# Two units of an output projection computed as one block with two sets of seven products

## The reference

```python
y = _rms(h, norm_mix_g[i])
z = y @ w_in[i]                       # 2048 x 4096
za, zb, zc, zd = jnp.split(z, split_at, axis=-1)
oa = _mixer_sgu(za, ...)              # spatial gating, 512 wide
ob = _mixer_shortconv(zb, sc_conv_w[i])
oc = _mixer_conformer(zc, ...)
od = _mixer_pool(zd, pool_w[i], pool_scale[i])
h = h + jnp.concatenate([oa, ob, oc, od], axis=-1) @ w_out[i]    # 2048 x 2048
y = _rms(h, norm_ffn_g[i])
h = h + (jax.nn.silu(y @ w_gate[i]) * (y @ w_up[i])) @ w_down[i]
...
h = h + jax.nn.sigmoid(y @ w_ple_gate[i]) * (p[i] @ w_ple_proj[i])
```

## Time and profile before

| | us |
|---|---|
| median of 3 runs | 1378.53 (1377.76 to 1378.97) |
| the profiled execution | 1376.73 |
| its span, first to last instruction | 1375.0 |
| TensorE busy (6169 matmuls) | 1369.3 |
| VectorE busy | 1156.1 |
| ScalarE busy | 885.2 |
| GpSimd busy | 151.3 |

### The profile page before, as it was taken

The page is one execution under the profiler, slowest core; times in us unless marked ns, Lnnn a source line. Parts: engine busy times, 40 slices in busy tenths (PEclk is TensorE's granted clock), DMA queues, the critical chain, the costliest instruction groups (busy, mean ns, idle before and its releaser), DMA issues.

```text
span 1375.0 us, 16935 instructions
## 1 busy us (share of the span) xinstructions
PE 1369.3 (100%) x6169; PEld 1122.6 (82%) x6169; DVE 1156.1 (84%) x1332; ACT 885.2 (64%) x1181; POOL 151.3 (11%) x129
## 2 busy tenths in 40 slices
PE   9999999999999999999999999999999999999998
PEld 7888888888888888888888888888888887777887
DVE  5589986687999988899999889988766769886898
ACT  7476755576777555777756576756666656665554
POOL 2000010011111000111100011100000144430000
PEclk9999999999999999999999999999999999999999
DMA  9776648887999788999987889998987878889686
GB/s 329 252 212 216 201 158 283 278 242 241 296 279 261 234 257 253 271 269 265 281 262 251 254 253 244 284 290 241 310 312 270 278 242 260 257 265 281 210 251 174
DMA packets 183146, 352.93 MB, mean 257 GB/s; under 512 B 13105, under 2 KB 37933, under 8 KB 182936
## 3 DMA queue, kind: packets, MB, share of 16 engines
q1 hardware_dynamic: 160408, 291.66, 64.5%
q0 software_dynamic: 9568, 35.02, 13.2%
q10 hardware_dynamic: 13088, 25.18, 6.1%
HBM read 296.19 MB, written 27.31 MB: 235 GB/s over the span
## 4 chain that ended last, share of the span: by engine, by line
PE 99%; DVE 0%; DMA 0%; ACT 0%; issue 0%; SPq 0%
PE acc L2216 14%; PE acc L2397 14%; PE acc L2400 14%; PE acc L2399 14%; PE acc L2217 14%; PE acc L2218 14%; PE sp L2400 2%; PE sp L2399 2%; PE tp L2400 2%; PE tp L2399 2%; PE sp L2397 2%; PE tp L2397 2%; PE acc L2278 1%; PE sp L2517 1%; PE tp L2533 1%; PE tp L2236 0%
## 5 line engine op out<-in xcount | busy, mean ns | idle before, releaser
L979 ACT ACTIVATE w_hi<-w_raw 128x1024 fp32r<-128x1024 f32 x451 | 472.1, 1056 | 294.8 <-PE acc L2218 188.0
L1419 DVE TENSOR_TENSOR w_lo<-w_raw,w_hi 128x1024 fp32r<-128x1024 f32 x429 | 519.1, 1225 | 131.6 <-ACT w_hi L979 128.7
L2216 PE MATMUL acc<-w_lo,hh 128*128 128x512 f32 x480 | 189.0, 394 | 0.0
L2218 PE MATMUL acc<-w_hi,hl 128*128 128x512 f32 x480 | 186.9, 389 | 0.0
L2217 PE MATMUL acc<-w_hi,hh 128*128 128x512 f32 x480 | 186.9, 389 | 0.0
L2397 PE MATMUL acc<-w_lo,yh 128*128 128x512 f32 x452 | 176.0, 389 | 0.0
L2399 PE MATMUL acc<-w_hi,yh 128*128 128x512 f32 x452 | 175.9, 389 | 0.0
L2400 PE MATMUL acc<-w_hi,yl 128*128 128x512 f32 x452 | 175.9, 389 | 0.0
L979 ACT ACTIVATE w_hi<-wide 128x1024 fp32r<-128x1024 f32 x108 | 114.3, 1060 | 69.6 <-DVE wide L1433 30.2
L1419 DVE TENSOR_TENSOR w_lo<-wide,w_hi 128x1024 fp32r<-128x1024 f32 x108 | 131.5, 1222 | 14.9 <-ACT w_hi L979 14.6
L2216 PE MATMUL acc<-w_lo,yh 128*128 128x512 f32 x352 | 137.4, 390 | 0.0
(11 more groups left out here) (333 smaller groups left out, 2227.6 us busy)
## 6 DMA issues: line engine op xcount, KB each, us to landing
w_raw<-in_w_gate SPq DMA_DIRECT2D x88, 512.0 KB, 5.8
w_raw<-in_w_up SPq DMA_DIRECT2D x88, 512.0 KB, 6.2
w_raw<-in_w_down SPq DMA_DIRECT2D x88, 512.0 KB, 6.4
w_raw<-in_w_in SPq DMA_DIRECT2D x64, 512.0 KB, 4.6
wide<-w_raw POOLq DMA_DIRECT2D x54, 512.0 KB, 5.9
w_raw<-in_swa_w_in ACTq DMA_DIRECT2D x48, 512.0 KB, 5.2
w_raw<-in_w_out SPq DMA_DIRECT2D x32, 512.0 KB, 5.8
w_raw<-in_w_ple_gate SPq DMA_DIRECT2D x32, 512.0 KB, 6.6
```

The source lines that it names most:

```text
L979: act.activation(w_hi[:, v % SPL], src, ACT.Copy).then_inc(hi_ready, 1)
L1419: dve.tensor_tensor(w_lo[:, v % SPL], src, w_hi[:, v % SPL].bitcast(F32), ALU.subtract).then_inc(lo_ready, 1)
L2216: pe.matmul(dst, xh[:, f, tk], w_lo[:, v % SPL, k], start=(f == 0), stop=False)
L2218: last = pe.matmul(dst, xl[:, f, tk], w_hi[:, v % SPL, k], start=False, stop=(f == CK * end + CK - 1))
```

## The change

Units 12 and 13 become the block `MIXED_PAIR` with quads 0 and 1 (the short convolution's features) and twelve plain chunks. Its places in the order of the engines (`MIXED_AT`) say when tops are copied, weights summed, input sums made and split, and the results mixed and added. The input sums of the block use `sum_h(0)` with `whole_first`, and the sums of the later blocks get the next numbers. The four stores of the parked projection go in front of the fetch of the turned spatial gate, after the block's eighth load, since its first `copy_tops` now is the first user of `wide`. The feed-forward turns of columns 0 and 1 move into units 14 and 15. `sum_y` works on two quads at a time, and the split of its sums is made in two halves with a wait of TensorE each.

```diff
+MIXED_PLAN = plain(0, 2, 3) + plain(1, 2, 3) + plain(0, 6) + quad("g", 0) + plain(1, 6) + quad("g", 1) + plain(0, 7)
+MIXED_PLAN += plain(1, 7) + quad("u", 0) + quad("t", 0) + quad("s", 0) + quad("u", 1) + plain(0, 4) + quad("t", 1)
+MIXED_PLAN += quad("s", 1) + plain(0, 5) + plain(1, 4, 5)
+MIXED_AT = dict(whole=1, sums=4, sums_high=6, sums_low=6, turned=8, m1=14, mix=18, mixed_gate=19, bank=19,
+                copied={6: [0], 7: [1]}, summed={0: 9, 1: 13})
...
+MIXED_PAIR = Block(OUT_UNIT, MIXED_PLAN, **MIXED_AT)
...
-            for j in range(NG):
+            b = MIXED_PAIR
+            for i, p in enumerate(b.loads):
+                role = int(p[0] == "u" or p[:2] == ("n", 1))
+                load(b.raw + i, wout_v, OUT_ROWS[p[-1]], CW * role)
+                if i == 7:
+                    put(T_OA)
+                    for j in range(NG):
+                        put_proj(j)
+                    fetch(T_OA)
+            for j in range(2, NG):
                 for c in range(8):
-                    load(START[OUT_UNIT + j] + c, wout_v, OUT_ROWS[c if j else OUT_FIRST[c]], CW * j)
-                    if (j, c) == (0, 7):
-                        move(T_OA)
-                    if j >= 2 and c == 4:
+                    load(START[OUT_UNIT + j] + c, wout_v, OUT_ROWS[c], CW * j)
+                    if (j, c) in ((2, 7), (3, 5)):
                         move(T_FFN + j - 2)
-                    if (j, c) in ((1, 3), (1, 7), (2, 7), (3, 3)):
-                        put_proj(((1, 3), (1, 7), (2, 7), (3, 3)).index((j, c)))
...
+            b = MIXED_PAIR
+            for i in range(len(b.plan)):
+                for q in b.at["copied"].get(i, ()):
+                    copy_tops(b, q)
+                split_high(b.v0 + i)
+                if i < 3:
+                    take(PROJ_UNIT + 1 + i, wide_v[:, :, CW * (i + 1):CW * (i + 2)], ACT.Copy, 1.0)
...
+                if i == b.at["turned"]:
+                    turned_high(T_OA, hh[:, 8:12])
+                if i == b.at["sums_high"]:
+                    h_sums_to_high(0)
+                if i == b.at["m1"]:
+                    copy_m1(b)
...
-                    if (j, c) == (3, 7):
-                        act.wait_ge(y_sums, 5)
-                        act.activation(y_sums_hi[:], gates[:, 0:TRIPLES].rearrange("p q (f n) -> p q f n", f=4),
-                                       ACT.Copy).then_inc(y_sums_high, 1)
+                    if (j, c) in ((2, 5), (3, 3)):
+                        ffn_turned_high(j - 2)
+                    if (j, c) == (3, 2):
+                        y_sums_to_high(0)
...
+            b = MIXED_PAIR
+            for i in range(len(b.plan)):
+                split_low(b.v0 + i)
...
+                if i == b.at["whole"]:
+                    whole_first()
...
+                if i == b.at["turned"]:
+                    turned_low(T_OA, hl[:, 8:12], hh[:, 8:12])
+                if i == b.at["sums"]:
+                    wait_half(dve, H_CN + 1)
+                    sum_h(0)
+                if i == b.at["sums_low"]:
+                    h_sums_to_low(0)
+                if i == b.at["mix"]:
+                    mix(b)
+                if i == b.at["mixed_gate"]:
+                    add_mixed_gate(b, 0)
+                if i == b.at["bank"]:
+                    add_bank(b, 0, 1)
+
+            for j in range(2, NG):
+                for c in range(8):
+                    split(START[OUT_UNIT + j] + c)
+                    if (j, c) == (2, 0):
+                        wait_left(dve, OUT_UNIT)
+                        turn(T_FFN, columns(0))
+                    if (j, c) == (2, 1):
+                        add_mixed_up(MIXED_PAIR, 1)
+                    if (j, c) == (2, 2):
+                        add_bank(MIXED_PAIR, 1, 2)
+                    if (j, c) in ((2, 5), (3, 3)):
+                        ffn_turned_low(j - 2)
...
+                    if (j, c) in ((2, 5), (3, 4)):
+                        wait_left(dve, OUT_UNIT + j - 1)
+                        turn(T_FFN + j - 1, columns(j - 1))
+                    if (j, c) in ((2, 6), (2, 7), (3, 0), (3, 1)):
+                        sum_y(0, {6: (0,), 7: (1, 2), 0: (3,), 1: (4,)}[c])
+                    if (j, c) == (3, 5):
+                        y_sums_to_low(0)
+                    if j == 3 and c >= 5:
+                        sum_y(1, {5: (0,), 6: (1, 2), 7: (3, 4)}[c])
...
+            def before_mixed(i, p):
+                if i == 0:
+                    pe.wait_ge(mix_ready, 1)
+                    wait_half_left(pe, H_PO + 1)
+                if p == ("n", 0, 6):
+                    pe.wait_ge(mix_ready, 2)
+                if p == ("g", 0):
+                    wait_half_left(pe, H_CN + 1)
+                    pe.wait_ge(oa_ready, 1)
+                if p == ("u", 0):
+                    pe.wait_ge(h_sums_low, 1)
+                if p == ("n", 0, 4):
+                    pe.wait_ge(turned_lo, T_OA + 1)
+
+            block(MIXED_PAIR, hh, hl, h_sums_hi, h_sums_lo, None, before_mixed)
+            for j in range(2, NG):
+                for c in range(8):
+                    chunk(START[OUT_UNIT + j] + c, OUT_UNIT + j, c, hh, hl)
```

More of the change, by code:

```diff
@@ L1136, in _, with y_sums_to_high, copy_m1 @@
             take(PROJ_UNIT, wide_v[:, :, 0:CW], ACT.Copy, 1.0)
-            for j in range(NG):
+            def y_sums_to_high(half):
+                q = slice(2 * half, 2 * half + 2)
+                act.wait_ge(y_sums, 5 * half + 5)
+                act.activation(y_sums_hi[:, q], gates[:, q].rearrange("p q (f n) -> p q f n", f=4),
+                               ACT.Copy).then_inc(y_sums_high, 1)
+            def copy_m1(b):
+                act.wait_ge(used, b.split("g", b.quads[-1]) + 1)
+                if b is PAIR[0]:
+                    act.wait_ge(y_sums_low, 2)
+                act.activation(gates[:, 0], tp[0][:], ACT.Copy).then_inc(m1_copied, 1)
@@ L1203, in pair @@
                     split_high(b.v0 + i)
+                    if m == 0 and i == 1:
+                        y_sums_to_high(1)
                     if i == b.at.get("low2"):
@@ new lines, in columns, with add_mixed_gate, add_mixed_up @@
+            def columns(d):
+                return resid[:, :, CW * d:CW * (d + 1)]
+            def add_mixed_gate(b, d):
+                dve.wait_ge(mixed_up, 3 * b.no)
+                if b.at["bank"] < b.at["mixed_gate"]:
+                    wait_left(dve, b.unit)
+                dve.tensor_tensor(columns(d), gates[:, 0:2], columns(d), ALU.add).then_inc(mixed_added, 1)
+            def add_mixed_up(b, d):
+                dve.wait_ge(mixed_up, 3 * b.no)
+                dve.tensor_tensor(columns(d), gates[:, 2:4], columns(d), ALU.add).then_inc(mixed_added, 1)
@@ new lines, in add_bank, with whole_first @@
+            def add_bank(b, d, after):
+                wait_unit(dve, b.unit + d % 2)
+                dve.wait_ge(mixed_added, after)
+                dve.tensor_tensor(columns(d), acc_pair[(b.unit + d) % 2][:], columns(d), ALU.add).then_inc(left["d"], 1)
+            def whole_first():
+                dve.tensor_tensor(tile[7][:], hh[:, 0:4].bitcast(F32).rearrange("p k n -> p (k n)"),
+                                  hl[:, 0:4].bitcast(F32).rearrange("p k n -> p (k n)"), ALU.add).then_inc(first_whole, 1)
@@ L1790, in add_bank @@
-            def add_bank(b, d, after):
-                wait_unit(dve, b.unit + d % 2)
-                dve.wait_ge(mixed_added, after)
-                dve.tensor_tensor(columns(d), acc_pair[(b.unit + d) % 2][:], columns(d), ALU.add).then_inc(left["d"], 1)
-            def whole_last():
-                dve.tensor_tensor(tile[7][:], hh[:, 0:4].bitcast(F32).rearrange("p k n -> p (k n)"),
-                                  hl[:, 0:4].bitcast(F32).rearrange("p k n -> p (k n)"), ALU.add).then_inc(last_whole, 1)
@@ L2361, in _ @@
                     to_features(H_CN, tok(4))
-            for j in range(NG):
-                for i in range(8):
-                    u, c = OUT_UNIT + j, i if j else OUT_FIRST[i]
-                    if j == 0 and c == 0:
-                        pe.wait_ge(mix_ready, 1)
-                        wait_half_left(pe, H_PO + 1)
-                    if j == 0 and c == 4:
-                        pe.wait_ge(turned_lo, T_OA + 1)
-                    if j == 0 and c == 6:
-                        pe.wait_ge(mix_ready, 2)
-                    chunk(START[u] + i, u, c, hh, hl, end=None if j else OUT_FIRST[-1])
             def third_sums_of(q, f):
@@ L2456, in before @@
                             pe.wait_ge(y_sums_low, 1)
+                    if m == 1 and p == ("u", 2):
+                        pe.wait_ge(y_sums_low, 2)
                 block(PAIR[m], yh, yl, y_sums_hi, y_sums_lo, None, before)
```

246 lines of the change are left out of this document (118 added, 128 removed).

## The result

| | before | after |
|---|---|---|
| median, 13 runs each, same chips | 1377.52 us (1376.61 to 1378.97) | 1380.26 us (1378.65 to 1383.18) |
| profiled execution, its span | 1375.0 us | 1377.1 us |
| TensorE | 6169 matmuls, 100% | 6163 matmuls, 99% |

A forecast was written before the change was run, and what follows sets the result against it. TensorE was taken as the bound, at 0.2267 us per matmul plus its waits. Profiled 1376.73 - 1.36 (six products) + 0.3 (stall) = 1375.7 us, plus 1.80 to the median: 1377.5 us; range 1376.4 to 1379.6.

The forecast's parts named there:

- The products: Units 12 and 13: 186 matmuls instead of 192, six fewer at 0.2267 us each, saving 1.36 us.
- The added wait for the stores: Before step 6 ScalarE's first copy of tops needs all four stores landed, between 212.9 and 216.0; no stall of step 6.
- the sum of transfers that puts load 9's landing at 218.1: Behind the turned tile (207.65): four stores at 1.3 us to 212.9, fetch 215.4, loads 8 and 9 at 216.7 and 218.1.
- SyncE's issues: Four stores at about 0.55 us each to issue, fetch 1.75 us, loads 8 and 9 issued some 0.5 us later than before.
- The accumulating transfer: First quad's transfer, issued near 214.9, delays load 9 by 0 to 1.3 us and load 10 by 1 to 3.
- step 8's date (221.4): Load 10 is wanted for step 8 by about 221.4 and lands at 219.4 if unhindered.
- The bound of 1.7 us on the stall: Upper bound for a late second copy before step 7: 218.1 + 2.6 - 219.0; lower bound 0, 0.3 us taken.
- The slower rival: Waiting for stores and loads makes ScalarE the bound at steps 6 and 7; up to 1384.1 us; chance 0.06 past 0.2%.
- the queue rival: Shared queue delays loads 9 and 10 by 1 to 2.5 us and the saving is spent: about 1378.9 us; chance 0.18.
- lower granted clock after such a wait: Listed sign that the prediction is wrong altogether, beside a TensorE wait elsewhere; no size given.
- The head, middle and end of the block, units 14 and 15: VectorE's work and the later turns cost nothing; end-of-block slack 0.5 us; rival of late VectorE additions 1378.5 us, chance 0.06.
- The round-robin case: DMA engines alternate between queues, so load 9 shares from 216 on and lands near 220: a stall of 1 us.

The follow-up runs named there:

- e4_add_waits: The changed kernel, but GpSimd issues the first accumulating transfer only when load 10 has landed: 1377.93 us, 1.0003 of before.
- e1_early_stores: The changed kernel with three of the four parking stores ahead of the turned tile's store: 1376.54 us, 0.9991 of before; run again 1376.45 us, 0.9995.
- e3_fetch_later: The changed kernel, but the turned tile is fetched after loads 8 to 10 instead of ahead of them: 1381.91 us, 1.0037 of before.
- e8_after_again: The changed kernel run once more, unaltered: 1380.84 us, 1.0023 of the kernel before.

## Why the prediction was wrong

- **The products: right.** 6163 matmuls. With the stall removed the medians are 0.7 and 0.9 us below before, not 1.36. All profiles of the kernels with the block but that of e4_add_waits have a wait between 813 and 820 us that the earlier trace rows's kernel lacks (0.4 us idle in the change, 0.5 and 0.4 with early stores, each some 0.16 more in delay), which would make up most of the rest. It stands behind an accumulating transfer of 8.3 instead of 7.6 us.
- **The added wait for the stores: right in kind.** The fourth store let the first copy go at 213.4 (forecast 213 to 216), without harm to step 6.
- **The step that failed: the sum of transfers that puts load 9's landing at 218.1.** It landed at 220.5, the second copy started at 220.5 instead of 218.1, and the deadline was 218.8 (the text has 219.0). From the fourth store to load 9 the sum has 5.2 us (212.9 to 218.1) and the trace 7.1 (213.3 to 220.5): the fetch of the turned tile's quarters 3.4 us where the sum has 2.5, load 8 2.0 and load 9 1.7 where it has 1.3 and 1.4. The four stores themselves took 6.0 us instead of 5.2, but began 0.3 us sooner. The pace of 1.3 us was read from loads that follow loads; behind stores and quarters the queue moved 227 to 234 GB/s and not the 400 that this pace means. With early stores, where the fetch is issued in 1.78 us, the same stretch takes 7.0 us, and in the kernel before it takes 7.7 from the fetch's first issue (207.67) to the second load's landing (issued 209.94, 5.4 us). So that trace had the sign of it. Why quarters and the first loads behind them move so slowly stays open.
- **SyncE's issues were mis-sized too, and are not shown to be the cause.** The prediction has four stores at 0.55 us each and the fetch at 1.75, and the loads 0.5 us later than before; they took 3.97 and 3.58 us, and the loads left 3.3 us later. But a load issued behind the stores at 209.12 still waited for them (e3_fetch_later), and the comparison under e1_early_stores shows no cost of its own. Long issues went with a full queue.
- **Slips in the text's own sums, none of which decides.** By its own terms load 9 lands at 207.65 + 5.2 + 2.3 + 2.6 = 217.8 and not 218.1. Seven transfers of 1.46 us behind 207.65 give 217.9, not "near 219". A stall of 2 us with the spread used at the lower end gives 1380.0, not 1379.3, as the end of the range.
- **The accumulating transfer: right in size, from a wrong start.** Load 10 was given a delay of 1 to 3 us and load 9 one of 0 to 1.3. By e4_add_waits it costs load 10 2.4 us (10.3 against 7.9) and load 9 0.2. But unhindered load 10 would have landed near 221.6 (an estimate: issued 213.71, 7.9 us as in e4_add_waits) and not at 219.4; with the delay it landed at 224.0, 2.6 us behind step 8's date (221.4).
- **The bound of 1.7 us on the stall: wrong**, since it starts from load 9 at 218.1 and looks at step 7 alone. Idle in the block was 2.5 us in two waits, and the delay about 2.8.
- **The slower rival** named this mechanism, place and deadline, but at 0.06 and past 0.2% only; the queue rival next to it had 0.18. Together they were the result. The point at which it passes 0.2% (second copy at 223.2) assumed a cost of one for one. The granted clock broke that in e8_after_again: the last bullet's "lower granted clock after such a wait" was listed as a sign and given no price.
- **The head, middle and end of the block, units 14 and 15: right.** VectorE's additions before unit 14 and the later turns caused no wait in any profile.
- **The round-robin case.** The Trainium skill ("DMA: Bandwidth & Descriptors", Queues, rings and completion order) says that a DMA engine takes turns between the queues that have work. The prediction took from it that load 9 would be slowed from 216 on, for a stall of 1 us. For load 10 the trace agrees: issued 1.1 us ahead of the accumulating transfer, it landed at 224.0, and that transfer at 224.4. For load 9 it doesn't: with the accumulating transfer held back its time from issue to landing fell by 0.2 us only.

## What to carry to other kernels

Bulk stores belong where the queue is idle, ahead of what the next stage waits for: the same four stores cost nothing with two or three of them 5 to 10 us earlier. When something is put into a busy queue, take the pace from a row with the same kinds of transfers in the same order, not from a row of loads alone, then hold the landing of each load behind it against the date by which it is wanted. In a kernel that is dense on TensorE a saving of six matmuls is smaller than one late load, and an idle stretch of 2 us can cost more than its own length again through the clock (3.4 us in e8_after_again, behind waits of 2.0 and 0.5 us).

## What the runs showed of the hardware

- In the change, issuing a 512 KB store took SyncE 0.6 us for the first two and about 1.3 us for the third and fourth, 3.97 us in all, and the fetch behind them took 3.58 us instead of 1.78 with early stores.
- The queue moved 380 GB/s with 512 KB stores (207 to 211 us of the change) and 227 to 234 GB/s with the 128 KB quarters and the first load behind them (213 to 217 us).
- Behind waits of TensorE of 2.0, 3.8, 4.0 and 4.5 us the granted clock fell to 0.50 in this place, and the matmuls ran 0.43 us apart (two starts at 225.66 and 226.09 in e8_after_again) instead of 0.23, for some 3 to 7 us. It didn't after waits of 1.4, 1.6 and 1.7 us.
- Load 10 took 10.3 us next to an accumulating transfer and 7.9 us with that transfer held back (e4_add_waits). Load 11 took 13 us next to two of them (e3_fetch_later).
